# One PEER block kernel: thirty-two late tokens by gathered rows instead of sixteen, a 352-column score product, seven residual tiles on VectorE, and a new timetable of gathers

## The chip, the cores and the metric

The kernel is one program on one core of a Trainium2 chip. The metric is device time in microseconds (us), the median of three runs. TensorE's granted clock is 0.999 of full speed in the profiled execution.

## The reference

One trunk layer on 512 tokens of width 1024: a mixer (Mamba-2 and differential attention, not touched here), then PEER, then a gate. PEER is where the change lies, and it is the larger part of the time:

```python
q  = (xt @ wq).reshape(PEER_BLOCK, PEER_HEADS, 2, PEER_HALF)     # 8 heads, two halves
v1, i1 = top_k(q[:, :, 0] @ sub_k1.T, 16); v2, i2 = top_k(q[:, :, 1] @ sub_k2.T, 16)
top, pos = top_k(v1[..., None] + v2[..., None, :], 16)            # eidx = i1 * 128 + i2
g   = softmax(top)                                                # 128 experts for each token
act = gelu(einsum("td,thkd->thk", xt, expert_u[eidx]))
h  += einsum("thk,thkd->td", act * g, expert_v[eidx])
```

There are 16384 experts, a row of U and a row of V of 1024 floats each.

## The kernel before, in words

The 512 tokens are treated in three ways.

**384 tokens are "dense" for V**, in `DT = 384` columns. For 128 tiles of U (`n_steps`), each of 128 experts and 512 KB, TensorE computes the scores of those experts for the tokens (`score_products`): 24 matmuls per tile with `DS` columns, in three times eight. Eight use the high part of U and the high part of the tokens (L396), eight the high part of U and the low part of the tokens (L397), and, after a wait for `lo_ready`, eight use the low part of U (L402). The high part is a cast by ScalarE (`split`, L1769), the low part (the residual, raw minus high) a subtraction by GpSimd, called POOL below (`low_part`, L1606). ScalarE applies GELU (L1774), and SP stores 192 KB of activations per tile to DRAM. `raw`, `hi` and `lo` are rings of four tiles. ScalarE issues `split(n+2)` ahead of `gelu(n)`, so that the order on ScalarE is gelu(n), split(n+3), and the cast of tile n+3 starts as soon as TensorE is through with tile n.

**128 tokens** (the first block) are treated by gathered rows: for each of 128 pairs (head, rank) POOL issues an indirect DMA that fetches one row of U for each token (512 KB), into a ring of eight rows (`U_RING`), and VectorE multiplies it by the token's row in PSUM and adds up (`dot`, L1890).

**The last `XT` of the dense tokens** have their scores from gathered rows too ("late" pairs). The 128 pairs of 16 tokens are packed, 8 pairs at a time, into the 128 partitions, which makes `XK = 16` further gathers and dots; these dots have both operands in SBUF (`s_hn_x`). The dense score product then has only `DS = DT - XT = 368` columns. The results go through DRAM (`xa_dram`) and come back turned by strided DMAs (`take_back`), into the weights of the last steps.

The order of work is written out by hand. `due(n)` is the number of gathers that POOL has issued once it is through with tile n: after each `low_part(n)` it issues gathers up to `due(n)`. Before a gather it waits for the dot that read the same ring place eight gathers ago. VectorE takes its dots in places of their own: some between the pieces of the retrieval of blocks 1 to 3 (`DOTS_T`), then a free run up to `in_a`, then four and five around the softmax.

Tiles 2 to 71 have no other work on TensorE than the scores (and nine transposes after tile 69). At tiles 72 to 119 (the loop stage, 48 steps) VectorE makes one-hot matrices for 8 tokens per step (8 of L2017 and one of L2019) and one or two dots, and TensorE multiplies the one-hots (`spread_and_score`, L1690) ahead of each tile. Tiles 120 to 127 are scores alone again. In that tail SP issues, in this order, the stores of activations, the loads of the last U tiles, and the first loads of the gate weights (`load_weights`). Then comes the value stage: 32 groups of four V tiles, 72 matmuls of 512 columns each (L1706), with the row gathers of V beside it.

Of the kernel before, what the change touches and what calls it, by code (L numbers as in the profile page):

```python
# [10 lines left out]
F32 = mybir.dt.float32  # L11
# [4 lines left out]
ALU = mybir.AluOpType  # L16
# [17 lines left out]
PAIRS = PH * TOPK  # L34
# [31 lines left out]
UR = 4  # L66
WARM = 13
U_FIRST = 4
# [6 lines left out]
LOOP_A = 72  # L75
EXP_AT, TURN_AT = 64, 68
FIRST_GATHER = 10
KEPT = 2
DT = T - P
U_RING, U_AHEAD = 8, 4  # L80
DOTS_T, DOTS_M, DOTS_J = (0, 8, 10, 10), 12, 12
DOTS_FREE = 32
DOTS_EXP, DOTS_PRE = 4, 9
XT = 16
XG = P // XT
XK = PAIRS // XG
DS = DT - XT

# [1281 lines left out]
def experts_and_embedding(nc, new_sem, shared, io, act_dram, gate_dram, h_dram, e_dram, hx_dram, xi_dram, xa_dram, out):  # L1370
# [8 lines left out]
    n_steps = NK  # L1379
    turns = n_steps // UR  # L1380
    n_body = DT // (8 * STEP_TOK)
    LOOP_C = LOOP_A + 8 * n_body
    OUTS = 2 * (TB - 1)
    with ExitStack() as ctx:
# [30 lines left out]
        raw, hi, lo = (shared[k] for k in ("raw", "hi", "lo"))  # L1415
# [89 lines left out]
        v_rows = io["v_t"].rearrange("i p d -> (i p) d")  # L1505
        ident, iota = con[:, K_ID:K_ID + P], con[:, K_IOTA:K_IOTA + P]

        block = ctx.enter_context(nc.Block())

        @block.sync  # L1510
        def _(sp):
# [18 lines left out]
            def load_scores(it, s):  # L1530
                sp.wait_ge(lo_ready[s], it)
                sp.dma_start(raw[:, s, :], io["u_t"][it * UR + s]).then_inc(tile_loaded[s], 16)
                store_acts(it * UR + (s - UR), s, it)
# [9 lines left out]
                    load_scores(it, s)  # L1543
            load_scores(turns - 1, 0)
            load_scores(turns - 1, 1)
            for tile in range(2):
                sp.wait_ge(gates_stored[tile], 16 * (n_body - 1))
            for s in range(UR):
                sp.wait_ge(act_stored[s], 16)
            load_weights(0, 0, 0)  # L1550
            load_scores(turns - 1, 2)
            load_scores(turns - 1, 3)
            for s in range(UR):
                load_value(0, s)
                if s == 1:
# [42 lines left out]
        def _(pool):  # L1598
# [20 lines left out]
                                        bounds_check=NK * NK - 1).then_inc(row_loaded[s], 16)  # L1619
                pair_no += 1  # L1620

            def due(n):

                if n < EXP_AT:
                    return max(0, min(3 * (n - FIRST_GATHER + 1) // 2, in_a * (n - FIRST_GATHER + 1 + U_AHEAD) // (EXP_AT - FIRST_GATHER), in_a))
                if n < LOOP_A:
                    return in_a + 3 + 11 * (n - EXP_AT) // 8
                return min(PAIRS + XK, in_a + DOTS_PRE + 3 * (n - LOOP_A + 3) // 2)

            for n in range(n_steps):  # L1630
                if n >= U_FIRST:
                    low_part(n)
                while pair_no < due(n):
                    gather()
# [129 lines left out]
        def _(act):  # L1764
# [46 lines left out]
                        act.wait_ge(gates_copied[1], 8 * j + k + 1)  # L1811
                        act.dma_start(gate_dram[2 * j + tile], gtile[:, tile, :, :]).then_inc(gates_stored[tile], 16)

            steps(0)
            steps(1)
            for s in range(U_RING):
                act.wait_ge(dotted[s], x_till // U_RING + (s < x_till % U_RING))
            act.activation(x_dots[:, :], x_dots[:, :], ACT.Gelu).then_inc(x_gelu, 1)
            act.wait_ge(x_gelu, 1)
            act.dma_start(xa_dram, x_dots[:, :]).then_inc(xa_stored, 16)  # L1820
            steps(2)
            act.wait_ge(xa_stored, 16)

            def take_back(g):
                act.dma_start(x_acts[g * XK:(g + 1) * XK, :], xa_dram[g * XT:(g + 1) * XT, :].rearrange("t k -> k t"), allow_slow_non_contiguous=True).then_inc(xa_back, 16)

            steps(3, also=take_back)
            with act.Fori(4, n_body - 1) as j:
                steps(j)
            steps(n_body - 1, keep=True)  # L1830
            with act.Fori(LOOP_C // UR, turns - 1) as it:
                for s in range(UR):
# [53 lines left out]
        def _(dve):  # L1886
# [13 lines left out]
            def dot_of_pair(q):  # L1900
                late = x_from <= q < x_till
                if q == x_from:
                    dve.wait_ge(hx_loaded, 16 * XG)
                dot(q % U_RING, q // U_RING + 1, hn_x[:, :] if late else hn_dot, col(x_dots if late else dots, row_of(q)[1]))
# [73 lines left out]
            for t in range(1, TB):  # L1978
                retrieve(t, sum(DOTS_T[:t]), DOTS_T[t])
            dve.tensor_copy(x_ids[:, :], expert).then_inc(x_known, 1)  # L1980
            for q in range(sum(DOTS_T), in_a):
                dot_of_pair(q)
            done = TB * OPS

# [260 lines left out]
```

## Time and profile before

| What | us |
|---|---|
| median of 3 runs (lowest to highest) | 1562.83 (1560.61 to 1564.15) |
| the profiled execution's own time | 1560.82 |
| its span, first to last instruction | 1559.1 |
| TensorE busy | 1537.4 |
| VectorE busy | 1154.6 |
| POOL busy | 1068.5 |
| ScalarE busy | 628.1 |

TensorE's busy time is the union of modelled matmul spans, so the pace of a stage is read from where one group of matmuls starts after another, not from this total. The stages in the span: mixer and retrieval scores to 390; tiles 2 to 71 to 672.5; loop stage to 950.4; tail to 983; values to 1506; the gate to the end.

### The profile page before, as it was taken

The numbers are of one execution on the slowest core, as the hardware profiler recorded it, in microseconds if no ns is written. First come the engines' busy times: TensorE is split into PE (matmuls) and PEld (weight loads), VectorE is DVE, ScalarE is ACT, GpSimd is POOL, SyncE is SP. The second block draws the span as 40 slices with busy tenths as digits, with TensorE's granted clock in tenths as the row PEclk, the third lists the DMA queues.
The fourth block names the chain that finished last, engine by engine and source line by source line (L and its number), as shares of the span: only waits on it lengthen the run. The fifth ranks groups of instructions, "written<-read, shape, count | busy, mean of one in ns | idle before, by whom it ended". The sixth has DMA issues, their size and how long they took to land.

```text
span 1559.1 us, 24881 instructions
## 1 busy us (share of the span) xinstructions
PE 1537.4 (99%) x8622; PEld 1385.3 (89%) x8622; DVE 1154.6 (74%) x2386; ACT 628.1 (40%) x945; POOL 1068.5 (69%) x562
## 2 busy tenths in 40 slices
PE   9999999999999999999999999999999999999998
PEld 8976887788999999999999999888888888888887
DVE  7897573777999933399999992568677676776855
ACT  5335752202333333456555654433333333333331
POOL 6543315554598999888666665788878878788763
PEclk9999999999999999999999999999999999999999
DMA  7222103422599999899999997999999999999961
GB/s 285 106 74 102 69 28 125 143 89 96 176 360 339 317 335 332 300 312 362 360 345 351 360 328 227 338 349 366 356 370 358 358 357 346 351 342 349 344 228 54
DMA packets 169140, 420.46 MB, mean 270 GB/s; under 512 B 15968, under 2 KB 90208, under 8 KB 164336
## 3 DMA queue, kind: packets, MB, share of 16 engines
q1 hardware_dynamic: 125856, 256.02, 46.9%
q0 software_dynamic: 39168, 142.62, 25.6%
q10 hardware_dynamic: 4048, 21.01, 3.4%
q8 instruction: 31, 0.51, 0.1%
q14 instruction: 37, 0.30, 0.1%
HBM read 367.08 MB, written 52.51 MB: 269 GB/s over the span
## 4 chain that ended last, share of the span: by engine, by line
PE 66%; DVE 6%; issue 1%; POOL 1%; DMA 1%; ACT 0%; POOLq 0%
PE psum L1706 34%; PE psum L402 8%; PE psum L397 8%; PE psum L396 8%; PE psum L1690 5%; PE psum L257 1%; PE psum L248 1%; PE psum L258 1%; DVE psum L1961 1%; DVE s_gtile L1957 1%; DVE s_gtile L1959 1%; DMA s_late_rows<-in_u_rows,s_u_row 1%; DVE psum L1929 0%; POOL u_lo L1606 0%; DVE s_late_rows L1890 0%
## 5 line engine op out<-in xcount | busy, mean ns | idle before, releaser
L1606 POOL TENSOR_TENSOR u_lo<-u_raw,u_hi 128x1024 fp32r<-128x1024 f32 x220 | 551.7, 2508 | 175.0 <-ACT u_hi L1769 170.9
L1769 ACT CAST u_hi<-u_raw 128x1024 fp32r<-128x1024 f32 x252 | 263.7, 1048 | 291.0 <-PE psum L1706 256.4
L396 PE MATMUL psum<-hn_hi,u_hi 128*128 128x368 f32 x1024 | 340.6, 333 | 2.1 <-PEq L138 2.1
L397 PE MATMUL psum<-hn_lo,u_hi 128*128 128x368 f32 x1024 | 336.4, 329 | 0.0
L1706 PE MATMUL psum<-u_hi,s_whi 128*128 128x512 f32 x768 | 298.0, 389 | 0.9 <-ACT acts L1774 0.9
L1706 PE MATMUL psum<-u_lo,s_whi 128*128 128x512 f32 x768 | 298.0, 389 | 0.0
L1706 PE MATMUL psum<-u_hi,s_wlo 128*128 128x512 f32 x768 | 297.9, 389 | 0.0
L396 PEld LDWEIGHTS psum<-hn_hi,u_hi 128*128 128x128 f32 x1024 | 192.3, 188 | 2.4 <-issue 2.4
L402 PE MATMUL psum<-hn_hi,u_lo 128*128 128x368 f32 x1024 | 191.8, 329 | 0.7 <-POOL u_lo L1606 0.7
L397 PEld LDWEIGHTS psum<-hn_lo,u_hi 128*128 128x128 f32 x1024 | 192.2, 188 | 0.0
L1639 POOL DMA_INDIRECT s_vrows<-in_v_t,s_v_row x128 | 162.3, 1268 | 26.1 <-issue 24.5
L1774 ACT ACTIVATE acts<-psum 128x368 f32<-128x368 f32 x126 | 60.3, 478 | 292.3 <-PE psum L402 257.9
L2066 DVE SCALAR_TENSOR_TENSOR psum<-s_vrows,s_w,psum 128x1024 f32<-128x1024 f32 x127 | 162.7, 1281 | 19.3 <-DMA s_vrows<-in_v_t,s_v_row 10.2
L402 PEld LDWEIGHTS psum<-hn_hi,u_lo 128*128 128x128 f32 x1024 | 173.2, 188 | 1.2 <-POOL u_lo L1606 1.0
L229 POOL TENSOR_SCALAR m_w_hi<-m_w_raw 128x2048 fp32r<-128x2048 f32 (+1 forms) x23 | 44.0, 1912 | 186.6 <-PE psum L248 156.5
L1706 PEld LDWEIGHTS psum<-u_hi,s_whi 128*128 128x128 f32 x768 | 144.1, 188 | 31.0 <-issue 1.1
L1706 PEld LDWEIGHTS psum<-u_lo,s_whi 128*128 128x128 f32 x768 | 144.1, 188 | 30.1
L1706 PEld LDWEIGHTS psum<-u_hi,s_wlo 128*128 128x128 f32 x768 | 144.1, 188 | 29.9
L2035 DVE TENSOR_TENSOR scores<-scores,s_gtile 128x256 f32<-128x256 f32 x32 | 52.2, 1632 | 147.8 <-DMA scores<-gate_scratch 143.1
L2017 DVE TENSOR_SCALAR scores<-psum,scores 128x128 f32<-128x128 f32 x384 | 126.6, 401 | 7.7 <-PE psum L1690 7.7
L1890 DVE CUSTOM_DVE_ANT_0 s_late_rows<-s_late_rows,psum 128x1024 f32<-128x1024 f32 x64 | 76.9, 1216 | 49.9 <-DMA s_late_rows<-in_u_rows,s_u_row 49.9
L231 POOL TENSOR_TENSOR m_w_lo<-m_w_raw,m_w_hi 128x2048 fp32r<-128x2048 f32 (+1 forms) x23 | 106.3, 4623 | 1.9
(344 smaller groups left out, 2644.7 us busy)
## 6 DMA issues: line engine op xcount, KB each, us to landing
u_raw<-in_u_t SPq DMA_DIRECT2D x128, 512.0 KB
u_raw<-in_v_t SPq DMA_DIRECT2D x128, 512.0 KB
act_scratch<-acts SPq DMA_DIRECT2D x128, 192.0 KB
scores<-act_scratch SPq DMA_DIRECT2D x32, 768.0 KB
gate_scratch<-s_gtile ACTq DMA_DIRECT2D x10, 2048.0 KB
scores<-gate_scratch SPq DMA_DIRECT2D x32, 640.0 KB
m_w_raw<-in_w_in SPq DMA_DIRECT2D x9, 1024.0 KB, 4.8
m_w_raw<-in_w_q SPq DMA_DIRECT2D x8, 1024.0 KB, 4.8
```

Source lines behind the costliest of these rows:

```text
L231: pool.tensor_tensor(lo, raw, hi.bitcast(F32), ALU.subtract).then_inc(self.lo_ready[s], 1)
L396: pe.matmul(out, hi[:, d * P:(d + 1) * P], dense(hn_hi, d), start=(d == 0), stop=False)
L397: pe.matmul(out, hi[:, d * P:(d + 1) * P], dense(hn_lo, d), start=False, stop=False)
L402: last = pe.matmul(out, lo[:, d * P:(d + 1) * P], dense(hn_hi, d), start=False, stop=(d == DC - 1))
L1606: pool.tensor_tensor(lo[:, s, :], raw[:, s, :], hi[:, s, :].bitcast(F32), ALU.subtract).then_inc(lo_ready[s], 1)
L1639: pool.indirect_dma_start(vrows[:, k, :], None, v_rows, bass.IndirectOffsetOnAxis(ap=v_row[:, n:n + 1], axis=0), bounds_check=NK * NK - 1) ...
L1690: last = pe.matmul(psG[:, half, n, :], onehot[:, par, 0, 4 * half + n, :], onehot[:, par, 1, 4 * half + n, :], start=True, stop=True)
L1706: return pe.matmul(outs[o], ww[:, par, s, t * P:(t + 1) * P], vv[:, s, half * 512:(half + 1) * 512], start=start, stop=stop)
L1769: act.copy(hi[:, s, :], raw[:, s, :]).then_inc(hi_ready[s], 1)
L1890: dve.tensor_tensor_reduce(rows[s], rows[s], by, 1.0, 0.0, ALU.mult, ALU.add, into)\
L2017: dve.tensor_scalar(onehot[:, par, 0, n, :], iota_ps, col(pair[:, 0, :], t0 + n), col(pair[:, 1, :], t0 + n), ALU.is_equal, ALU.mult)
L2066: dve.scalar_tensor_tensor(hn_dot, vrows[:, k, :], w, hn_dot, ALU.mult, ALU.add).then_inc(vrow_added[k], 1)
```

## The change

- `XT` goes from 16 to 32. The dense product has 352 columns, there are 32 late gathers and dots instead of 16 (160 in all instead of 144), packed four pairs at a time; four `take_back` DMAs instead of eight, of twice the tokens each.
- `DOTS_FREE` goes from 32 to 38, so `in_a` goes from 60 to 66. The late dots take places 78 to 109 of the order of dots instead of 72 to 87, and ScalarE waits for them after the third round of `steps` instead of the second. The rest of those rounds is moved back by one.
- `due(n)` is new. Up to tile 41 it goes one gather per tile (two at tiles 11, 13, 24 and 41), from 42 to 63 it makes 30 gathers in 22 tiles, from 64 to 119 it has the cadence of before (12 in the eight tiles 64 to 71, then three per two tiles), and 10 gathers are left for tiles 120 to 125. Before, tiles 14 to 59 had about 1.11 per tile, 60 to 63 none and 120 to 127 none.
- The residuals of tiles 44, 47, 50, 53, 56, 59 and 62 (`DVE_LOW`) are made by VectorE. In its order they stand ahead of dot `due(n - 1)`, that is right behind the dot of the last gather that POOL issues at tile n-1.
- SP loads the last two U tiles ahead of its wait for the gates and of the first load of gate weights, and stores the activations in their places after it.

```diff
-DOTS_FREE = 32
+DOTS_FREE = 38
 DOTS_EXP, DOTS_PRE = 4, 9
-XT = 16
+FREE_AT = 41
+DVE_LOW = tuple(range(44, 64, 3))
+XT = 32
...
+        def due(n):
+
+            first = sum(DOTS_T) + U_RING
+            if n <= FREE_AT:
+                return max(0, min(3 * (n - FIRST_GATHER + 1) // 2, first * (n - FIRST_GATHER + 3) // (FREE_AT - FIRST_GATHER + 3)))
+            if n < EXP_AT:
+                return first + (in_a - first) * (n - FREE_AT) // (EXP_AT - 1 - FREE_AT)
+            if n < LOOP_A:
+                return in_a + 3 + 11 * (n - EXP_AT) // 8
+            if n < LOOP_C:
+                return in_a + DOTS_PRE + 3 * (n - LOOP_A + 3) // 2
+            return min(PAIRS + XK, in_a + DOTS_PRE + DOTS_J * n_body + 4 + 2 * (n - LOOP_C))
...
             load_scores(turns - 1, 1)
+            for s in range(2, UR):
+                sp.wait_ge(lo_ready[s], turns - 1)
+                sp.dma_start(raw[:, s, :], io["u_t"][n_steps - UR + s]).then_inc(tile_loaded[s], 16)
             for tile in range(2):
                 sp.wait_ge(gates_stored[tile], 16 * (n_body - 1))
             for s in range(UR):
                 sp.wait_ge(act_stored[s], 16)
             load_weights(0, 0, 0)
-            load_scores(turns - 1, 2)
-            load_scores(turns - 1, 3)
+            for s in range(2, UR):
+                store_acts(n_steps - 2 * UR + s, s, turns - 1)
...
             for n in range(n_steps):
-                if n >= U_FIRST:
+                if n >= U_FIRST and n not in DVE_LOW:
                     low_part(n)
...
-            steps(0)
-            steps(1)
+            for j in range(3):
+                steps(j)
...
-            steps(2)
+            steps(3)
             act.wait_ge(xa_stored, 16)
...
-            steps(3, also=take_back)
-            with act.Fori(4, n_body - 1) as j:
-                steps(j)
+            steps(4, also=take_back)
             steps(n_body - 1, keep=True)
...
+            def low_part(n):
+
+                s, it = n % UR, n // UR
+                dve.wait_ge(hi_ready[s], it + 1)
+                dve.wait_ge(tile_used[s], it)
+                dve.tensor_tensor(lo[:, s, :], raw[:, s, :], hi[:, s, :].bitcast(F32), ALU.subtract).then_inc(lo_ready[s], 1)
+
             for q in range(sum(DOTS_T), in_a):
+                for n in DVE_LOW:
+                    if q == due(n - 1):
+                        low_part(n)
                 dot_of_pair(q)
```

## Rows read from the trace of the kernel before

**Rows 1.** The chain that ended last, in order of time: start, us, what.

```profile
650.35 1.33 PE psum L402 x8
654.35 1.33 PE psum L402 x8
...
672.68 1.78 PE psum L1690 x16
677.13 1.33 PE psum L402 x8
...
682.92 1.33 PE psum L402 x8
...
983.31 522.52 PE psum L1706 x2304
```

**Rows 2.** Busy time by window: its us, PE, PEld, DVE, ACT, POOL, clock, DMA, GB/s.

```profile
464.00:472.00 8.00, 8.00 (x50) 7.92 (x49) 7.97 (x59) 3.46 (x5) 7.62 (x5) 1.00 1.00 386
...
550.00:664.00 114.00, 114.00 (x688) 113.97 (x687) 41.61 (x65) 43.49 (x60) 101.90 (x60) 1.00 0.92 323
672.00:820.00 148.00, 148.00 (x1028) 148.00 (x1027) 147.31 (x316) 89.33 (x105) 111.52 (x66) 1.00 0.94 344
...
946.00:983.00 37.00, 36.44 (x220) 36.13 (x219) 7.01 (x10) 15.40 (x22) 21.62 (x9) 1.00 0.76 253
983.00:1506.00 523.00, 522.69 (x2308) 432.82 (x2309) 372.54 (x264) 179.85 (x162) 420.66 (x226) 1.00 0.98 347
```

**Rows 3.** Timeline of POOL, tiles 14 and 32 to 33.

```profile
436.77 2.40 POOL L1606 TENSOR_TENSOR u_lo<-u_raw,u_hi 128x1024 fp32r<-128x1024 f32 x1
...
510.65 2.42 POOL L1606 TENSOR_TENSOR u_lo<-u_raw,u_hi 128x1024 fp32r<-128x1024 f32 x1
513.23 1.04 POOL L1618 DMA_INDIRECT s_late_rows<-in_u_rows,s_u_row  x1 [0.16 <-issue]
514.58 1.01 POOL L1618 DMA_INDIRECT s_late_rows<-in_u_rows,s_u_row  x1 [0.30 <-issue]
515.61 2.42 POOL L1606 TENSOR_TENSOR u_lo<-u_raw,u_hi 128x1024 fp32r<-128x1024 f32 x1
519.25 2.42 POOL L1606 TENSOR_TENSOR u_lo<-u_raw,u_hi 128x1024 fp32r<-128x1024 f32 x1
```

**Rows 4.** Timeline of TensorE: residual products of tiles 2, 33 and 64.

```profile
393.07 0.33 PE L402 MATMUL psum<-hn_hi,u_lo 128*128 128x368 f32 x1
```
```profile
518.08 0.43 PE L402 MATMUL psum<-hn_hi,u_lo 128*128 128x368 f32 x1 [0.68 <-POOL u_lo L1606]
```
```profile
642.19 0.49 PE L402 MATMUL psum<-hn_hi,u_lo 128*128 128x368 f32 x2
```

**Rows 5.** Timeline of POOL, tile 64: its residual and three gathers.

```profile
633.21 2.40 POOL L1606 TENSOR_TENSOR u_lo<-u_raw,u_hi 128x1024 fp32r<-128x1024 f32 x1 [1.60 <-ACT u_hi L1769]
635.76 1.04 POOL L1618 DMA_INDIRECT s_late_rows<-in_u_rows,s_u_row  x1 [0.15 <-issue]
...
638.42 1.01 POOL L1618 DMA_INDIRECT s_late_rows<-in_u_rows,s_u_row  x1 [0.30 <-issue]
```

**Rows 6.** Timeline of VectorE: dots of the first and third of those gathers.

```profile
642.49 1.22 DVE L1890 CUSTOM_DVE_ANT_0 s_late_rows<-s_late_rows,psum 128x1024 f32<-128x1024 f32 x1 [16.64 <-DMA s_late_rows<-in_u_rows,s_u_row]
...
646.33 1.22 DVE L1890 CUSTOM_DVE_ANT_0 s_late_rows<-s_late_rows,psum 128x1024 f32<-128x1024 f32 x1 [0.58 <-DMA s_late_rows<-in_u_rows,s_u_row]
```

**Rows 7.** The value stage's residuals on VectorE: ns min/median/max, first and last start.

```profile
L2072 DVE TENSOR_TENSOR u_lo<-u_raw,u_hi x32: 1208/1213/2495, 985.2 to 1490.7; 128x1024 fp32r<-128x1024 f32 x32
```

**Rows 8.** Timeline of POOL, tile 69's gather, and VectorE after it.

```profile
657.91 1.31 POOL L1618 DMA_INDIRECT s_late_rows<-in_u_rows,s_u_row  x1 [0.16 <-issue]
```
```profile
664.81 1.22 DVE L1890 CUSTOM_DVE_ANT_0 s_late_rows<-s_late_rows,psum 128x1024 f32<-128x1024 f32 x1 [1.93 <-DMA s_late_rows<-in_u_rows,s_u_row]
```

**Rows 9.** Timeline of VectorE in the loop stage, late dots.

```profile
727.81 1.98 DVE L1890 CUSTOM_DVE_ANT_0 s_late_rows<-s_late_rows,s_hn_x 128x1024 f32<-128x1024 f32 x1
...
734.54 2.59 DVE L1890 CUSTOM_DVE_ANT_0 s_late_rows<-s_late_rows,s_hn_x 128x1024 f32<-128x1024 f32 x1
737.07 0.08 DVE L1890 DVE_READ_ACCUMULATOR2_ANT s_x_dots<- 128x1 f32 x1
737.07 2.63 DVE L2017 TENSOR_SCALAR scores<-psum,scores 128x128 f32<-128x128 f32 x8
739.63 1.20 DVE L2019 TENSOR_TENSOR scores<-con,psum 128x1024 f32<-128x1024 f32 x1
740.76 1.21 DVE L1890 CUSTOM_DVE_ANT_0 s_late_rows<-s_late_rows,s_hn_x 128x1024 f32<-128x1024 f32 x1
```

**Rows 10.** Timeline of POOL in the loop stage, same stretch.

```profile
733.65 2.41 POOL L1606 TENSOR_TENSOR u_lo<-u_raw,u_hi 128x1024 fp32r<-128x1024 f32 x1 [1.64 <-ACT u_hi L1769]
```

**Rows 11.** The tail: SP's first weights load, VectorE's use of it.

```profile
960.01 0.57 SPq L1528 DMA_DIRECT2D scores<-gate_scratch  x1
```
```profile
966.95 0.43 DVE L2035 TENSOR_TENSOR scores<-scores,s_gtile 128x256 f32<-128x256 f32 x1 [26.89 <-DMA scores<-gate_scratch]
```

More of the change, by code:

```diff
@@ L1620, in gather @@
                 pair_no += 1
[L1622 to L1628, printed above, removed]
             for n in range(n_steps):
-                if n >= U_FIRST:
+                if n >= U_FIRST and n not in DVE_LOW:
                     low_part(n)
@@ L1820, in _ @@
             act.dma_start(xa_dram, x_dots[:, :]).then_inc(xa_stored, 16)
-            steps(2)
+            steps(3)
             act.wait_ge(xa_stored, 16)
             def take_back(g):
+                if g >= XG:
+                    return
                 act.dma_start(x_acts[g * XK:(g + 1) * XK, :], xa_dram[g * XT:(g + 1) * XT, :].rearrange("t k -> k t"), allow_slow_non_contiguous=True).then_inc(xa_back, 16)
-            steps(3, also=take_back)
-            with act.Fori(4, n_body - 1) as j:
-                steps(j)
+            steps(4, also=take_back)
             steps(n_body - 1, keep=True)
```

## The prediction

> **What bounds the kernel now.** I first read the chain of work that ended last. From tile 2 to the value stage it is TensorE alone, at a constant pace: a score tile every 4.00 us outside the loop stage, a step every 5.79 us in it, and the 2304 matmuls of the value stage in 522.52 us [rows 1]. The windows by stage say the same: TensorE is busy all the time from 550 to 820 [rows 2]. They also show who is near behind. Up to tile 71 POOL is busy 101.90 of 114 us, in the first half of the loop stage VectorE is busy 147.31 of 148 us, and the 16 DMA engines show a share of 0.92 to 0.98 in every stage but the tail [rows 2]. So a cheaper score tile gives time directly, until POOL, VectorE or the DMA engines take over. Then I read the timelines of POOL and TensorE side by side, to see how far ahead each residual is of the matmul that needs it.
>
> **The gain on TensorE.** A matmul's pitch is 4.00 us / 24 = 166.7 ns at 368 columns and 522.52 / 2304 = 226.8 ns at 512 columns [rows 1]: 0.418 ns per column, so 16 columns less are 6.7 ns less, 160.0 ns, and a tile takes 3.84 us, 0.16 less. Is there a floor? The 16 matmuls of 128 columns take 1.78 us, 111 ns each [rows 1]. A line from there to 368 columns has only 0.23 ns per column, which would give 0.09 us per tile. I take 0.16, because 352 lies next to the 368 and in line with the 512, and keep 0.09 as the low end. Tiles 2 to 127 are 126: 126 x 0.16 = 20.2 us (low end 11.3). The value stage keeps its 512 columns and its number of matmuls, and gains nothing.
>
> **POOL up to tile 43.** POOL takes 519.25 - 515.61 = 3.64 us for a residual and one gather, and 515.61 - 510.65 = 4.96 us with two: 1.3 us for the second [rows 3]. Before, tile 33's residual was ready at 518.03 and TensorE waited 0.68 us for it; its product came 0.9 us late against the 4.00 us grid (393.07 + 31 x 4.00 = 517.07) [rows 3, 4]. The new timetable has four gathers fewer by tile 33, so this 0.9 us goes. At the new pace, tile 14 is the tight one: its residual is ready at 436.77 + 2.40 = 439.17 [rows 3], its product is wanted at 393.07 - 0.1 + 12 x 3.84 = 439.0. That is 0.1 us of wait. From there on POOL gains 3.84 - 3.65 = 0.19 us per tile and loses 1.3 at each of the two doubles (24 and 41), so at tile 43 it is 29 x 0.19 - 2.6 = 2.9 us ahead. VectorE's ten dots per retrieved block find their rows in time either way, since their gathers are 10 us or more ahead of them.
>
> **Seven residuals on VectorE.** Here a new wait arises. VectorE makes residual n behind the dot of the last gather of tile n-1. Count from the end e of POOL's residual n-1. The gather starts at e + 0.16. Its row comes 6.7 us later when it is the first of a burst (635.76 to 642.49), and the dot of the third began 7.9 us after its issue (638.42 to 646.33) [rows 5, 6]. Bursts of three it will be, as POOL, relieved of residual n, goes straight on to the gathers of tile n. Then 1.15 us for the dot and 1.21 us for the residual [rows 6, 7]: e + 9.2 after a single gather (n = 44, 47, 50), and e + 0.16 + 1.34 + 7.3 + 2.4 = e + 11.2 after a double (53, 56, 59, 62). When is it wanted? With POOL in full lead the residual n-1 is ready 6.2 us ahead of its product. (Tile 64 shows 642.19 - 635.61 = 6.6 [rows 4, 5]; over two tiles the new pace takes 0.3 of it.) One tile of 3.84 us on top makes e + 10.0. So the singles just pass, the doubles miss by 1.2 us. Tile 44 is worse, as POOL's lead there is only 2.9: wanted at e + 6.7, ready at e + 9.2, a miss of 2.5. A miss also gives the next of the seven, three tiles on, that much more room, since the cast it hangs on is tied to an earlier tile. So I count 2.5 at 44, 1.2 at 53, 1.2 at 59. To this comes the port. A late dot in the loop stage, with both operands in SBUF, that begins while POOL makes a residual ends one dot's length after that residual: 734.54 took 2.59 us, ending at 737.13, where POOL's residual ended at 736.06 [rows 9, 10]. VectorE's residuals in the value stage go up to 2.50 us beside their median of 1.21 for the same reason [rows 7]. I add 0.6 on three of them, some 2 us. Sum: 7 us. Bounds: if rows come in 5 us, about 0.5 (tile 44 alone); if in 8 and the port is always taken, 12.
> The Trainium skill, in SBUF — State Buffer, section Who interferes with whom, says that a VectorE instruction with two SBUF inputs and a GpSimd instruction that reads SBUF exclude each other for the whole instruction. The rows on the late dots agree. By the rule alone each of the seven would wait up to a whole residual of POOL.
>
> **Gathers and DMA, tiles 42 to 71.** Between two of the seven POOL makes two residuals and four or five gathers, some 10.5 us of its 11.5, and stays in lead. From 64 to 71 it is over its pace by 12 gathers: 8 x 3.65 + 4 x 1.3 = 34.4 us against 31.7 with the transposes. It has the lead for that. A tile moves 524 KB of U, 197 KB of activations and 1.36 x 524 KB of rows, 1.44 MB: 374 GB/s at 3.84 us. The most that eight microseconds show is 386 GB/s at a share of 1.00, and the mean of long stretches is 323 to 347 [rows 2]. The stalls above stretch the mean tile to some 4.07 us and the demand down to 353 GB/s. So I cost the DMA engines at nothing beyond the 7 us, and keep them as a rival.
>
> **The start of the loop stage.** VectorE's first one-hot waits for dot 74, whose row is gathered at tile 69. Before, that gather went out at 657.91 and the dot began at 664.81 [rows 8], after which copies and a one-hot set (3.7 us) ended 1.7 us ahead of TensorE's need at 672.7 [rows 1]. Before, POOL was 4.4 us ahead at tile 69. Now the two gathers of tile 63 and the twelve after it leave 2.0, so all this comes 2.4 us later against TensorE, and TensorE's own need comes 0.4 earlier. I count 1.2 us (0 to 3).
>
> **The late dots in the loop stage.** Without contention VectorE needs per step 740.76 - 737.07 = 3.69 us for the one-hots and 1.5 dots of 1.15: 5.42 us [rows 9]. The new step is 5.79 - 0.16 = 5.63. The stretch by POOL's residuals is some 0.46 per step on average (over the eleven steps with late dots), which makes 5.88, more than TensorE's step. There are now 21 such steps instead of 11. I expect this to hold itself in check. As VectorE falls back, its first dot slides behind the end of POOL's residual, as at 740.76, which took 1.21 [rows 9], and the stretch is gone. I count 1 us; nothing (0) and 21 x 0.25 = 5 us are its ends.
>
> **The tail.** Ten gathers fall on tiles 121 to 125. POOL loses 1.1 us per tile of a lead of 6.2: hidden. They add 5.2 MB to a stage that runs at a share of 0.76 [rows 2]; the first weights, issued at 960.01 and used at 966.95 [rows 11], are wanted only by ScalarE's cast around 979.8, so some 10 us cover the later load, as they do for the two U tiles that are put ahead. The last dots end some 1 us ahead of the cast. 0.5 us (0 to 3). Nothing is gained here by the order of SP's loads, since TensorE's pitch was 4.00 us before. The 4-byte `take_back` packets double to 4096; they ride beside the gathers and I cost them at nothing, as the loop stage has DMA share to spare (0.94) [rows 2].
>
> **Sum.** -20.2 - 0.9 + 0.1 + 7 + 1.2 + 1 + 0.5 = -11.3 us. Against the profiled execution's 1560.82 that is 1549.5. The median of the runs is 2.0 higher, so the median should be 1551.5.
>
> **The rivals.**
> - Nothing new waits: the rows come in 5 us, and VectorE's slack is enough. Then -20.2 - 0.9 + 1, 1542.7 on the scale of the median. For it: TensorE never waits today. Against: tile 44's margin. 0.15.
> - The DMA engines bound tiles 42 to 71. If they give no more than 350 GB/s, these tiles need 22 x 1.44 + 8 x 1.51 = 43.7 MB, 125 us, where TensorE needs 116: 9 us. The loop stage moves 2.03 MB per step (a quarter of a 2.1 MB gate store besides), 5.79 us at 350 GB/s: nothing gained there at the worst. With 9 us and half of the loop stage's 7.9 lost, besides the 2.7 of the last three terms, the gain is some 5 us: 1558. For it: shares near 1. Against: 386 GB/s in eight microseconds [rows 2]. 0.2. The Trainium skill (DMA: Bandwidth & Descriptors, section Bandwidth) puts the HBM limit of a core at about 358 GB/s; by that figure the case would be an estimated 2 us better. The row with 386 exceeds it.
> - Slower: VectorE becomes the bound of the loop stage. If each late first dot meets a whole residual, as the one that took 2.59 did, it is stretched by 1.38: a step takes 6.80, 1.17 over TensorE's, 25 us over 21 steps, which ends at 1565 with the rest at its small end. It decides from about 1.0 per step. Against: it happened once in eleven. 0.06.
> - My forecast: 0.5. The rest, 0.09, goes to a mix near no change (residuals missing by 3 us each).
>
> The range 1543 to 1560 leaves out part of the first, of the worst DMA case and the slow side. Measurements can tell about 0.2% (3.1 us) here. Faster by more: 0.83; within: 0.1; slower: 0.07.
>
> **What would show it.** Matmuls of L402 with 352 columns in groups 3.84 us apart, 5.63 in the loop stage. TensorE waiting for VectorE's residual at tile 44 by 2 us or more, and at some of the others. VectorE's residuals longer than 1.3 us where POOL is in one. TensorE waiting for VectorE's one-hot at step 0. If TensorE has no waits, or if ScalarE's casts wait for U tiles by many microseconds (the DMA case), or if TensorE waits for one-hots all through tiles 74 to 95, I am wrong in that step.

## The result: slower by 0.3%, and where the time of the profiled execution went

| | before | after |
|---|---|---|
| median of 22 runs each (lowest to highest), us | 1561.77 (1560.49 to 1567.72) | 1567.33 (1561.90 to 1569.49) |
| ratio, 95% interval | | 1.0027 [1.002, 1.0034] |
| profiled execution, own time and span, us | 1560.82, 1559.1 | 1568.41, 1566.6 |

The forecast was 1551.5, the range 1543 to 1560. It was wrong, with its sign. I go by the profile: what TensorE waits for, where on its time line that lies, and what the engine waited for was doing.

First TensorE's waits in the kernel after (engine, line, tile, what it waited for: us in total, times, longest). Before, none of these four waits was above 0.9 us in sum.

```profile
PE psum L404 <- DVE u_lo L1996: 11.9, 4, 6.6
PE psum L1716 <- ACT acts L1784: 4.3, 1, 4.3
PE psum L404 <- POOL u_lo L1624: 2.8, 3, 1.4
PE psum L1700 <- DVE scores L2039: 2.8, 1, 2.8
```

L404 is the residual product (L402 before), L1996 VectorE's new residual, L1700 the product with the one-hots (L1690 before), L1716 the value stage (L1706 before).

The chain that ended last, near the end of the tail (start, us, what). It answers to [rows 1].

```profile
941.73 1.28 PE psum L404 x8
...
947.36 1.28 PE psum L404 x8
...
960.67 1.28 PE psum L404 x8
964.51 1.29 PE psum L404 x8
966.31 4.01 SPq L1529
970.36 6.81 SPq L1529
978.22 7.94 DMA u_raw<-in_v_t
989.32 524.08 PE psum L1716 x2304
```

The pace is as forecast: 964.51 - 960.67 = 3.84 us per tile, and in the loop stage 947.36 - 941.73 = 5.63. But the chain leaves TensorE for two stores on SP's queue and the transfer of a V tile. The value stage begins at 989.32 instead of 983.31, and its 2304 matmuls take 524.08 us instead of 522.52 [rows 1].

The windows of the kernel after, which answer to [rows 2] (its us, PE, PEld, DVE, ACT, POOL, granted clock, DMA share, GB/s):

```profile
550.00:664.00 114.00, 102.06 (x608) 100.91 (x609) 63.27 (x89) 37.63 (x53) 86.65 (x56) 0.96 0.91 323
560.00:570.00 10.00, 5.61 (x21) 5.61 (x22) 7.84 (x10) 1.40 (x2) 7.08 (x5) 0.66 0.79 282
672.00:820.00 148.00, 145.19 (x1026) 144.49 (x1025) 144.16 (x313) 86.11 (x102) 123.84 (x70) 1.00 0.95 351
946.00:983.00 37.00, 37.00 (x238) 37.00 (x237) 12.84 (x22) 13.11 (x18) 28.06 (x18) 1.00 0.93 333
988.00:992.00 4.00, 2.68 (x6) 2.15 (x7) 3.36 (x2) 1.16 (x3) 2.18 (x1) 0.65 1.06 388
```

From 550 to 664 TensorE is busy 102.06 of 114 us, and its mean clock is 0.96: some of the waits are followed by a stretch at the lower level of 1.2 GHz. Followed tile by tile (start of one residual product after the other, against 3.84 and 5.63), the span divides so:

| Term | forecast, us | profiled executions, us |
|---|---|---|
| narrower products, tiles 2 to 127 | -20.2 | -20.0 |
| the wait at tile 33 | -0.9 | -0.9 |
| tiles 11 to 41 | +0.1 | +3.0 |
| tiles 42 to 71, with the seven residuals | +7 | +18.5 |
| start of the loop stage | +1.2 | +3.0 |
| late dots in the loop stage | +1 | +0.4 |
| tail and start of the value stage | +0.5 | +5.0 |
| tile 2 starts earlier (391.75 for 393.07) | 0 | -1.3 |
| sum | -11.3 | +7.7 (the spans differ by 7.5) |

**Tile 44**, the largest piece, in the kernel after. First POOL (start, us, what, the idle time before it and what ended it):

```profile
542.48 1.04 POOL L1636 DMA_INDIRECT h<-in_u_rows,s_u_row  x1 [0.16 <-issue]
546.39 1.01 POOL L1636 DMA_INDIRECT s_more_row<-in_u_rows,s_u_row  x1 [2.87 <-DVE s_dots L1900]
...
551.03 2.43 POOL L1624 TENSOR_TENSOR u_lo<-u_raw,u_hi 128x1024 fp32r<-128x1024 f32 x1
553.62 1.04 POOL L1636 DMA_INDIRECT s_late_rows<-in_u_rows,s_u_row  x1 [0.16 <-issue]
```

Then VectorE, and TensorE's residual products of tiles 43 and 44:

```profile
546.75 0.29 DVE L1990 CAST s_x_ids<-psum 128x128 uint32<-128x128 int32 x1
...
560.20 1.22 DVE L1900 CUSTOM_DVE_ANT_0 s_late_rows<-s_late_rows,psum 128x1024 f32<-128x1024 f32 x1 [2.22 <-DMA s_late_rows<-in_u_rows,s_u_row]
561.35 0.08 DVE L1900 DVE_READ_ACCUMULATOR2_ANT s_dots<- 128x1 f32 x1
561.35 2.99 DVE L1996 TENSOR_TENSOR u_lo<-u_raw,u_hi 128x1024 fp32r<-128x1024 f32 x1
```
```profile
553.80 1.44 PE L404 MATMUL psum<-hn_hi,u_lo 128*128 128x352 f32 x8
564.39 2.72 PE L404 MATMUL psum<-hn_hi,u_lo 128*128 128x352 f32 x8 [6.59 <-DVE u_lo L1996]
```

Read from the bottom. The product of tile 44 was wanted at 553.80 + 3.84 = 557.6 and waited until 564.39. The residual ended at 561.35 + 2.99 = 564.34. With e, the end of POOL's residual 43, at 551.03 + 2.43 = 553.46, it was ready at e + 10.9, where I had e + 9.2: the row came after 560.20 - 553.62 = 6.6 us as expected, but the residual took 2.99 us instead of 1.21. It was wanted at e + 4.2, where I had e + 6.7: POOL's lead of 2.9 us had gone at tile 42, where its gather stood 2.87 us for a place in the ring, that is for a dot of VectorE. And VectorE was late because the last instruction of its retrieval (L1990, L1980 before) began at 546.75, not at 536.44 as before. I call that start the end of the retrieval below.

Why that? The small subtraction in the retrieval (two operands in SBUF), four times, in the kernel before (L1950) and after (L1960); ns min/median/max, first and last start:

```profile
L1950 DVE TENSOR_TENSOR s_found<-s_gtile x4: 284/346/1144, 403.9 to 513.6; 128x128 f32<-128x128 f32 x4
```
```profile
L1960 DVE TENSOR_TENSOR s_found<-s_gtile x4: 1527/2772/3299, 402.7 to 520.9; 128x128 f32<-128x128 f32 x4
```

An instruction of 0.28 us takes up to 3.30. The second of the four, beside POOL:

```profile
440.43 3.28 DVE L1960 TENSOR_TENSOR s_found<-s_gtile 128x128 f32<-128x128 f32 x1
```
```profile
440.06 1.04 POOL L1636 DMA_INDIRECT s_late_rows<-in_u_rows,s_u_row  x1 [0.16 <-issue]
441.12 2.42 POOL L1624 TENSOR_TENSOR u_lo<-u_raw,u_hi 128x1024 fp32r<-128x1024 f32 x1
```

Each of the four ended 0.1 to 0.2 us after the end of a residual of POOL. Two of them (2.27 and 1.53 us) began inside that residual. The two longest (3.28 and 3.30 us) began 0.7 us ahead of it, while POOL was in a gather; why they didn't get through in that time stays open, since one in the kernel before took 0.29 us beside a gather. In sum the four took 10.4 us instead of 2.1, and all dots of a late block behind them are late as well.

**The tail** of the kernel after: SP's issues, and ScalarE behind them.

```profile
962.85 1.18 SPq L1563 DMA_DIRECT2D u_raw<-in_u_t  x2
964.28 0.39 SPq L1542 DMA_DIRECT2D scores<-act_scratch  x1
964.72 0.79 SPq L1543 DMA_DIRECT2D scores<-gate_scratch  x1
966.31 10.86 SPq L1529 DMA_DIRECT2D act_scratch<-acts  x2
977.22 0.46 SPq L1533 DMA_DIRECT2D u_raw<-in_v_t  x1
```
```profile
984.38 1.05 ACT L1779 CAST u_hi<-u_raw 128x1024 fp32r<-128x1024 f32 x1 [6.57 <-DMA u_raw<-in_v_t]
985.33 0.46 ACT L1784 ACTIVATE acts<-psum 128x352 f32<-128x352 f32 x1
```

SP stands 10.86 us in the issue of two stores (a single one took 0.34 to 0.36 at the same place before). V tile 0 goes out at 977.22 (before: 967.37), its cast waits 6.57 us, and the activations of tile 126 and all else the value stage needs stand behind that cast in ScalarE's order.

### The profile page after: what moved, and what is told of

Read it like the earlier page. It is cut to its first block, busy times and chain, and to the rows that moved or that the text cites. A ratio compares the mean times of both kernels' runs of the same rounds, so it can differ in the third digit from the quotient of the medians.

```text
span 1566.6 us, 24934 instructions
## 1 busy us (share of the span) xinstructions
PE 1525.1 (97%) x8622; PEld 1370.3 (87%) x8622; DVE 1195.9 (76%) x2425; ACT 627.3 (40%) x945; POOL 1079.2 (69%) x571
## 4 chain that ended last, share of the span: by engine, by line
PE 56%; DVE 10%; issue 3%; DMA 3%; POOL 2%; SPq 1%; ACT 0%; POOLq 0%
PE psum L1716 33%; PE psum L1700 6%; PE psum L404 5%; PE psum L399 5%; PE psum L398 5%; DVE s_gtile L1967 1%; DVE psum L1971 1%; DVE s_gtile L1969 1%; DVE s_late_rows L1900 1%; DMA h<-in_u_rows,s_u_row 1%; PE psum L259 1%; PE psum L250 1%; PE psum L260 1%; DMA s_late_rows<-in_u_rows,s_u_row 1%; DVE h L1900 1%
## 5 line engine op out<-in xcount | busy, mean ns | idle before, releaser
L1624 POOL TENSOR_TENSOR u_lo<-u_raw,u_hi 128x1024 fp32r<-128x1024 f32 x213 | 529.7, 2487 | 162.9 <-ACT u_hi L1779 159.3
L398 PE MATMUL psum<-hn_hi,u_hi 128*128 128x352 f32 x1024 | 333.7, 328 | 2.1 <-PEq L140 2.1
L399 PE MATMUL psum<-hn_lo,u_hi 128*128 128x352 f32 x1024 | 329.6, 324 | 0.0
L1716 PE MATMUL psum<-u_hi,s_whi 128*128 128x512 f32 x768 | 299.3, 391 | 4.3 <-ACT acts L1784 4.3
L1716 PE MATMUL psum<-u_lo,s_whi 128*128 128x512 f32 x768 | 298.3, 389 | 0.0
L1716 PE MATMUL psum<-u_hi,s_wlo 128*128 128x512 f32 x768 | 298.0, 389 | 0.0
L404 PE MATMUL psum<-hn_hi,u_lo 128*128 128x352 f32 x1024 | 188.1, 326 | 14.7 <-DVE u_lo L1996 11.9
L1649 POOL DMA_INDIRECT s_vrows<-in_v_t,s_v_row x128 | 167.3, 1307 | 27.7 <-issue 24.2
L404 PEld LDWEIGHTS psum<-hn_hi,u_lo 128*128 128x128 f32 x1024 | 169.0, 190 | 17.0 <-DVE u_lo L1996 13.1
L1716 PEld LDWEIGHTS psum<-u_hi,s_whi 128*128 128x128 f32 x768 | 144.8, 189 | 34.7 <-issue 4.6
L1716 PEld LDWEIGHTS psum<-u_lo,s_whi 128*128 128x128 f32 x768 | 144.5, 188 | 30.0
L1716 PEld LDWEIGHTS psum<-u_hi,s_wlo 128*128 128x128 f32 x768 | 144.1, 188 | 30.1
L1784 ACT ACTIVATE acts<-psum 128x352 f32<-128x352 f32 x126 | 58.5, 464 | 277.3 <-PE psum L404 277.3
L2055 DVE TENSOR_TENSOR scores<-scores,s_gtile 128x256 f32<-128x256 f32 x32 | 46.2, 1443 | 131.7 <-DMA scores<-gate_scratch 131.7
L1816 ACT COPY s_gtile<-psum 128x512 f32<-128x512 f32 x96 | 100.2, 1156 | 2.5 <-PE psum L1700 2.5
```

Source lines behind the costliest of these rows:

```text
L398: pe.matmul(out, hi[:, d * P:(d + 1) * P], dense(hn_hi, d), start=(d == 0), stop=False)
L399: pe.matmul(out, hi[:, d * P:(d + 1) * P], dense(hn_lo, d), start=False, stop=False)
L404: last = pe.matmul(out, lo[:, d * P:(d + 1) * P], dense(hn_hi, d), start=False, stop=(d == DC - 1))
L1624: pool.tensor_tensor(lo[:, s, :], raw[:, s, :], hi[:, s, :].bitcast(F32), ALU.subtract).then_inc(lo_ready[s], 1)
L1649: pool.indirect_dma_start(vrows[:, k, :], None, v_rows, bass.IndirectOffsetOnAxis(ap=v_row[:, n:n + 1], axis=0), bounds_check=NK * NK - 1) ...
L1716: return pe.matmul(outs[o], ww[:, par, s, t * P:(t + 1) * P], vv[:, s, half * 512:(half + 1) * 512], start=start, stop=stop)
```

## The experiments

Each is timed beside the kernel before on the same chip; ratios are to that, with their 95% interval. The times of one kernel spread more than before's do, so that one profile is not its median; where I speak of an effect's size, it comes from the ratios.

**One part alone: 352 columns.** The kernel before with

```diff
+DM = 352
...
-    dense = lambda t, d: t[:, d, P:P + DS]
+    dense = lambda t, d: t[:, d, P:P + DM]
```

and the same width in PSUM and in the activations.

> The kernel before with 352 instead of 368 columns in the score product and its GELU, and nothing else of the change. It leaves out the scores of 16 tokens, whose activations are set to one. If the pitch of the matmuls follows the columns, score tiles come every 3.84 us and the ceiling of the gain is 20 us; POOL's timetable of before is too dense for that pace up to tile 20, so I expect TensorE to wait some 3 us there and the run to be 14 to 17 us faster than before. If instead the DMA engines are the next bound (rival), the tiles from 14 to 71 keep a pace near 3.95 to 4.0 us and the run is less than 8 us faster.

Measured: 1549.51 us (1547.67 to 1552.95), 0.9919 [0.9902, 0.9937]. The pitch is 3.84. From tile 2 to 127 it is 11.1 us shorter than before, not 20: the timetable of before, at the new pace, makes TensorE wait for POOL in seven of the tiles 12 to 33 (4.8 us, and some 2.6 us more beside these waits). So a new timetable was needed, but the columns alone, with the old one, were worth 12.7 us, less than the 14 to 17 expected and more than the rival's 8. The rest of the change, with the sixteen late gathers that this run leaves out, takes more than that back.

**Who makes the residuals.** The kernel after with POOL making all of them:

```diff
-DVE_LOW = tuple(range(44, 64, 3))
+DVE_LOW = ()
```

> The changed kernel with all residuals on POOL and the same timetable of gathers. POOL needs 22 x 3.65 + 8 x 1.3 = 91 us for tiles 42 to 63 and has 84 plus its lead. If VectorE's lateness (theory: its retrieval ends 10 us later, and its residuals stand behind the dots) costs 16 us in tiles 44 to 60, this run waits instead some 3 to 8 us for POOL and is 8 to 12 us faster than the changed kernel, so 4 to 8 us faster than before. If the late rows and full DMA queues are the cause whoever makes the residuals (rival), ScalarE's casts wait for U tiles and the time stays within 3 us of the changed kernel.

Measured: 1560.34 us (1555.37 to 1567.52), 0.9988 [0.9971, 1.0005]. TensorE waits 5.7 us for POOL, in eight tiles. So giving seven residuals to VectorE, in the places they have, made the kernel some 6 us slower than leaving them with POOL (8 to 12 were expected).

**Where they stand in VectorE's order.** The kernel after with each residual behind the dot of the last gather of tile n-2:

```diff
-                    if q == due(n - 1):
+                    if q == due(n - 2):
```

> The changed kernel with VectorE's residual n in front of dot due(n-2) instead of due(n-1), so one tile's gathers less stand before it. Theory (the place in VectorE's order costs the time): the waits at tiles 50, 53 and 59 go (6 us and the 1.7 us of lower clock after 59), the one at 44 shrinks from 6.6 us by one or two dots to about 4 to 5, and the run is 6 to 9 us faster than the changed kernel. Rival (the port is what holds VectorE's residuals): nearly the same waits, within 2 us of it.

Measured: 1554.77 us (1551.55 to 1560.40), 0.9958 [0.9945, 0.9971]: 0.69% below the ratio of after, 10.8 us. TensorE's waits in this kernel:

```profile
PE psum L1716 <- ACT acts L1784: 4.7, 1, 4.7
PE psum L1700 <- DVE scores L2039: 3.1, 1, 3.1
...
PE psum L404 <- POOL u_lo L1624: 1.4, 2, 0.8
```

No wait for a residual of VectorE is left among them (0.3 us are lost at tile 44). It wasn't VectorE's load that cost the time, but the place: behind a row that was asked for only 4 us before the residual was wanted (553.62 for 557.6 at tile 44). This run also shows how much the DMA engines give in these tiles:

```profile
550.00:664.00 114.00, 113.05 (x704) 112.44 (x702) 73.75 (x96) 45.93 (x62) 99.70 (x63) 1.00 1.00 373
```

TensorE keeps its pace with 373 GB/s at a share of 1.00. What is left stands at the start of the loop stage and of the value stage. At the first one the tile took 6.1 us too long with a wait of 3.1: in the windows behind it the granted clock is 0.53 for 5 us, then 0.79.

```profile
665.00:670.00 5.00, 3.71 (x17) 3.71 (x18) 5.00 (x12) 1.70 (x2) 4.50 (x4) 0.53 0.89 316
670.00:675.00 5.00, 5.00 (x28) 5.00 (x27) 5.00 (x12) 1.14 (x2) 3.50 (x3) 0.79 0.70 219
```

**The order of loads in the tail.** The kernel after with the last two U tiles loaded in their old places:

```diff
-            for s in range(2, UR):
-                sp.wait_ge(lo_ready[s], turns - 1)
-                sp.dma_start(raw[:, s, :], io["u_t"][n_steps - UR + s]).then_inc(tile_loaded[s], 16)
...
-            for s in range(2, UR):
-                store_acts(n_steps - 2 * UR + s, s, turns - 1)
+            load_scores(turns - 1, 2)
+            load_scores(turns - 1, 3)
```

> The changed kernel with SP's order of before in the tail: the last two U tiles behind the first weights. Theory: it is the ten gathers in the tail that fill the queues, and the order matters little: SP still stands at a store, the value stage starts within 1 us of the changed kernel's. Rival: the two U tiles ahead of the weights block SP's queue; without them the value stage starts some 3 us earlier, and the run is 3 to 5 us faster than the changed kernel.

Measured: 1572.74 us (1562.09 to 1576.63), 1.007 [1.005, 1.0089], 0.43% or 6.7 us slower than after; both theories had it equal or faster. Its profiled execution was the shortest of six and shows how: the load stands 6.95 us in SP's issue, ScalarE's cast of tile 126 waits, and behind it TensorE waits 4.1 us in the tail.

```profile
972.08 1.04 ACT L1776 CAST u_hi<-u_raw 128x1024 fp32r<-128x1024 f32 x1 [9.69 <-DMA u_raw<-in_u_t]
```

So this part of the change is worth something, in a kernel that has gathers in the tail.

**The port.** The kernel after with the small subtraction's first operand copied to PSUM ahead of it:

```diff
-                did(dve.tensor_tensor(found[:, t, 2, :].rearrange("p (h k) -> p h k", h=PH), top[:, :, :],
+                did(dve.tensor_copy(leftf[:, :, :], top[:, :, :]))
+                me.settle()
+                did(dve.tensor_tensor(found[:, t, 2, :].rearrange("p (h k) -> p h k", h=PH), leftf[:, :, :],
...
```

> The changed kernel, with the small subtraction of the retrieval (128 x 128, both inputs in SBUF, 10.4 us for four of them in the changed kernel's profile, 2.1 before) fed by a copy in PSUM instead, so that it has one input in SBUF. Theory (a port shared with POOL makes these four wait, and the 10 us of delay of the retrieval are what makes TensorE wait 6.6 us at tile 44): each of the four takes under 0.4 us, the retrieval ends by 540, the wait at tile 44 is under 2 us, and the run is 6 to 9 us faster than the changed kernel. Rival (the retrieval is late because its rows come late): the subtractions are short, the dots wait for DMA instead, and tile 44 waits as before.

Measured: 1565.44 us (1560.05 to 1568.29), 1.002 [1.0009, 1.0032]. The four subtractions took 0.29 us each, and the retrieval ended at 538.96. TensorE's wait at tile 44 fell from 6.59 to 3.8, but not away:

```profile
PE psum L404 <- DVE u_lo L1998: 8.8, 3, 3.8
```

The mechanism is shown, its weight is small: the ratio is 0.0007 (about 1 us) below that of after, inside the intervals, where 6 to 9 us were expected. The profiles suggest why: the stretch comes and goes. In this stretch of the time line the work is the same in after and in seven of the experiments. The retrieval ended at 546.75 in after and at 547.46 in one of them (activations first), at 543.37 with POOL making all residuals, and between 536.15 and 538.23 in the other five. The four subtractions took up to 3.29 us in the second, and none took more than 2.35 in the other six. So the profile of after shows one of the bad cases, and the copy can only give what the mean of them costs.

**The tail's gathers.** The kernel after without the last eight (head, rank) pairs of the first 128 tokens.

```diff
-            return min(PAIRS + XK, in_a + DOTS_PRE + DOTS_J * n_body + 4 + 2 * (n - LOOP_C))
+            return min(PAIRS + XK - 8, in_a + DOTS_PRE + DOTS_J * n_body + 4 + 2 * (n - LOOP_C))
...
```

> The changed kernel without the last eight of its gathers and dots, which leaves 2 of 10 gathers for tiles 120 to 125. It leaves out eight of the 128 pairs of the first 128 tokens. Theory (these gathers fill the DMA queues, SP stands 11 us in an issue, and the first V tile comes late): the value stage starts 1 us after the last score instead of 4.3, without the lower clock, and the run is 4 to 6 us faster than the changed kernel. Rival (the two U tiles ahead of the weights do it): the wait stays above 3 us.

Measured: 1562.42 us (1555.80 to 1568.07), 1.0004 [0.9987, 1.0021]: 0.23% or 3.6 us below after, with intervals that just touch. SP's issue of the two stores shrinks from 10.86 to 4.20, V tile 0 goes out at 966.95, and the wait at L1716 falls to 0.9, the value of before. From 960 to 980 the DMA share is 0.98 with 320 GB/s, where after has 1.05 and 390 from 966 to 983.

```profile
962.71 4.20 SPq L1529 DMA_DIRECT2D act_scratch<-acts  x2
966.95 0.43 SPq L1533 DMA_DIRECT2D u_raw<-in_v_t  x1
```

**The start of the loop stage.** Residuals two tiles earlier as above, and the last two dots ahead of the loop stage put behind the first one-hot set:

```diff
-            for q in range(in_a + DOTS_EXP, in_a + DOTS_PRE):
+            for q in range(in_a + DOTS_EXP, in_a + DOTS_PRE - 2):
...
+                if step_no == 0:
+                    for q in range(c0 - 2, c0):
+                        dot_of_pair(q)
```

> The kernel of the run two tiles earlier, with the last two dots ahead of the loop stage put behind its first set of one-hots. There TensorE waited 3.1 us for VectorE at step 0 and ran at half clock for 4 us after it, 6.1 us in all. Theory (the one-hots stand behind a dot whose row comes late): this goes to 0 to 1 us, and the run is 4 to 6 us faster than that one, near 1549. Rival (VectorE is simply full there): the wait comes back at step 1 to 3, less than 2 us are gained.

Measured: 1551.67 us (1547.92 to 1554.72), 0.9935 [0.9921, 0.995], 3.6 us below the kernel with the earlier residuals alone, with intervals that just touch. The wait went from step 0 (3.1 us) to step 3 (2.5 us), with 2 us less lost in all. So a different order moves the wait more than it removes it; that VectorE simply has too much to do in the first steps fits that, but wasn't tried by itself. Another cause that fits stands in the kernel after, just ahead of this place:

```profile
676.00:680.00 4.00, 4.00 (x27) 4.00 (x26) 2.72 (x7) 1.52 (x2) 3.81 (x3) 1.00 1.04 411
```
```profile
677.24 1.22 DVE L1900 CUSTOM_DVE_ANT_0 h<-h,psum 128x1024 f32<-128x1024 f32 x1 [1.48 <-DMA h<-in_u_rows,s_u_row]
```

The DMA engines are at a share of 1.04 with 411 GB/s, and the row of the last dot ahead of the one-hots, gathered at 669.68, was there 7.6 us later, where the forecast had 6.9. No run takes this load away. With the copy to PSUM as well:

> The one before, with the subtraction fed from PSUM as well. Theory: where the retrieval happened to run free of POOL, this adds nothing in the profile, but it takes out the chance of it, so that the times of all runs lie closer together and their median is 0 to 4 us lower. Rival (the port has no part in the spread): spread and median as without it.

Measured: 1552.27 us (1548.54 to 1554.27), 0.9941 [0.9928, 0.9954]. Not told apart from the one before.

**Why V tile 0 is late.** On that basis, once with the load of V tile 0 ahead of the two stores on SP, and once with ScalarE's activations of tile 126 ahead of the cast of V tile 0:

```diff
+            load_value(0, 0)
             for s in range(2, UR):
                 store_acts(n_steps - 2 * UR + s, s, turns - 1)
...
```
```diff
             for s in range(UR):
+                if s == 2:
+                    gelu(turns - 1, s)
                 split(turns - 1 + (s + 2) // UR, (s + 2) % UR)
...
```

> The kernel of the run before (residuals two tiles earlier, first one-hot set ahead of two dots; ratio 0.9935, profiled span 1549.5 us), and besides SP issues the load of V tile 0 ahead of the last two stores of activations instead of behind them. Theory A (the wait at the start of the value stage is V tile 0 that lands late, because its issue stands on SP behind stores that the ten tail gathers hold up): V tile 0 is issued at about 951 instead of 960.3 us, ScalarE's cast of it starts as soon as its buffer is free, and the wait of 3.2 us with about 1 us of lower clock behind it goes: 3 to 4 us less, ratio 0.9910 to 0.9915. Theory B (the DMA engines themselves are full there, the order on SP does not matter): the load is issued earlier and lands at 966 or later all the same, no change, ratio 0.9935.

> The same kernel as the basis (ratio 0.9935), and besides ScalarE makes the activations of tile 126 ahead of the cast of V tile 0 instead of behind it. Theory A (V tile 0 is late, and all of ScalarE's work behind it: two casts of V, one of weights, the activations of tile 127): only one activation of 0.46 us leaves the row behind the late cast, so the wait goes from 3.2 to some 2.7 us, ratio 0.993 to 0.9935. Theory C (the wait is made by ScalarE's order, the activations of tile 126 behind a cast that waits for its tile): the wait goes almost whole, 3 us less, ratio 0.9915.

Measured: 1552.95 us, 0.9945 [0.9929, 0.996], and 1553.24 us, 0.9940 [0.9922, 0.9958]. Neither helps. In the first, SP's issue and ScalarE's cast were:

```profile
950.96 0.34 SPq L1533 DMA_DIRECT2D u_raw<-in_v_t  x1
951.35 7.29 SPq L1529 DMA_DIRECT2D act_scratch<-acts  x3
```
```profile
965.03 1.05 ACT L1781 CAST u_hi<-u_raw 128x1024 fp32r<-128x1024 f32 x1 [4.25 <-DMA u_raw<-in_v_t]
```

The load goes out 9.3 us earlier than in its basis (960.29) and is there 2.4 us earlier (965.03 for 967.45), 14 us after its issue; 1.2 of the 2.4 is only that all of this execution lies that much ahead. So it isn't SP's order. The windows of the tail point to what it is: the 20 us up to the last residual product in this kernel (966.56) and in the one before the change (980.94).

```profile
946.00:966.00 20.00, 20.00 (x126) 20.00 (x125) 7.12 (x11) 5.89 (x10) 14.74 (x9) 1.00 1.04 388
```
```profile
960.00:980.00 20.00, 20.00 (x122) 20.00 (x121) 5.31 (x9) 7.30 (x11) 12.01 (x6) 1.00 0.93 311
```

A share of 1.04 with 388 GB/s for 20 us, where the kernel before had 0.93 with 311: the DMA engines are full. That what is issued there waits for them is a reading; the run with eight gathers less, in which the wait went, bears it out. In the second, ScalarE's activations of tile 126 waited 4.00 us for the store of tile 122's, which lay in the same jam.

**All four together** (earlier residuals, one-hots first, copy to PSUM, both orders of the tail):

> Residuals two tiles earlier, first one-hot set ahead of two dots, the retrieval's subtraction fed by a copy in PSUM, V tile 0 loaded ahead of the stores, activations of tile 126 ahead of the cast of V tile 0. If the four causes add up as the single runs show them, only the wait for one-hots at tile 75 (2.3 us) and the start waits are left: span about 1543, time about 1546, ratio 0.990. If something else takes over at the start of the value stage (the weights, or V tiles 2 and 3 behind the stores), 1549 or more.

Measured: 1550.33 us (1546.48 to 1552.41), 0.9922 [0.9906, 0.9937], the lowest of the kernels that compute the whole result, though its interval overlaps those of the four before it. The four edits do not add up to the 0.990 expected; TensorE's two large waits stay:

```profile
PE psum L1718 <- ACT acts L1786: 3.8, 1, 3.8
PE psum L1702 <- DVE scores L2046: 2.1, 1, 2.1
```

That is 1.05% faster than the changed kernel and 0.78% faster than before, as much as the narrower columns alone gave (0.9919, with the scores of 16 tokens left out).

## Why the prediction was wrong, step by step

- **The gain on TensorE**: right. The pitch is 160 ns at 352 columns, no floor, 20 us.
- **POOL up to tile 43**: the step that failed first. The wait at tile 33 went, as said. But "VectorE's ten dots per retrieved block find their rows in time either way" looked at rows only, not at when VectorE gets to its dots. A dot that comes late holds a place of the ring, and through it POOL. The lead of 2.9 us was 0.3 when tile 44 came (553.80 - 553.46). Tiles 11 to 15 cost 2.3 us instead of 0.1, with waits for POOL of 0.78 and 0.62; with the small subtraction fed from PSUM they cost 0.4 and, with all four edits, 0.6, so they too seem to come from the port.
- **Seven residuals on VectorE**: the mechanism was right (residual behind a row of the tile before, port on top), and the size was off, 18.5 for 7 us in the profile. At tile 44, 6.75 for 2.5: 2.5 of it from the lead, 1.7 from the port. At 53 and 59, 2.6 for 1.2 each. Tile 42, where the lead went, took 1.6 too long, and tile 50 0.6. 4.0 us is what no term of mine had: the lower clock behind the waits at 44 and 59. The port itself made the seven residuals 7.4 us longer in sum than seven times 1.21, where I had added 2. With the retrieval on time (the run with the copy) the wait at 44 was still 3.8. By the ratios the place alone is worth 10.8 us, and VectorE's part in the residuals, as placed, costs 6 us more than it saves. This is the term that was mis-sized most.
- **The start of the loop stage**: 3.0 for 1.2, at the upper end of its bounds. The first one-hot set began at 679.64. The gathers ahead of it are as many as I counted; the last of their rows took 7.6 us for 6.9, and by the experiment, order gives back only a part.
- **Late dots in the loop stage**: right. 0.4 us for 1; the pace of 5.63 held, and VectorE stayed busy 144.16 of 148 us. The slower rival, which needed a stretch of each step, did not occur: the kernel is slower, for which I had 0.07, but not on the way that I had named for it.
- **The tail**: failed. I spread 5.2 MB over a stage at a mean share of 0.76, but its second half had been at 0.91 before already (966 to 983). After, the gathers go out from 947 to 973, and their end meets the weights, two U tiles and V tile 0: the share from 966 to 983 is 1.05, with 390 GB/s. The stores and V tile 0 stood in that jam, and with eight of the ten gathers left out the wait fell from 4.3 to 0.9 us. "Some 10 us cover the later load" named the cover for the weights, not for V tile 0, which had none. 3.4 us until the value stage starts, and 1.6 of lower clock in it. "Nothing is gained here by the order" failed too: the old order costs 6.7 us more.
- **The DMA rival** did not occur in tiles 42 to 71 as I had put it: ScalarE's casts waited 1.3 us in all for U tiles from 550 to 664, and with the residuals two tiles earlier these tiles kept the pace with 373 GB/s, above the 350 of the rival. The loop stage kept its pace with 351 GB/s at a share of 0.95. Full engines showed in the tail (390 GB/s at 1.05) and for some microseconds ahead of the loop stage (411 at 1.04). The 2 us that I gave in this rival for the second, higher rate was low: 43.7 MB take 2.8 us less by it.

Two things stay open. The difference was to be -11.3 us. The medians differ by +5.6, and the ratio 1.0027 makes it +4.2; I go by the ratio, as for the experiments, so 15.5 us are to be explained. The place of the residuals (10.8), the one-hots (3.6) and the tail's gathers (3.6) make 18.0 us where I had 7, 1.2 and 0.5: 9.3 of the 15.5. The copy to PSUM gives about 1 more. Some 5 us are not placed by any run. Each of these terms has an interval of a few microseconds, so part of the 5 may be spread. And no run tried fewer bytes in the tail with the whole result computed.

## What to carry to other kernels

When work is given to an engine that has slack, ask where in its order it stands, and what the instruction ahead of it waits for: here the place was worth more than the work. A ring ties its two users together in both directions, so a consumer that is late by some microseconds takes the lead of the producer. And the mean DMA share of a stage says nothing of its last 20 us; count what must land there, and what goes out ahead of it.

## What the runs showed of the hardware

- TensorE's granted clock fell to the lower level after some waits: after 6.59 us at tile 44 it was 0.50 from 564 to 568, after 4.3 us 0.65 from 988 to 992. After the wait of 2.46 us at tile 59 it was 0.72 from 632 to 636, after one of the same 2.46 us at tile 53 it stayed, and so it did after 2.76 us at the start of the loop stage (1.00 from 684 to 694). So the length of a wait alone does not tell. Each fall cost 1.6 to 3 us. The wait of 3.1 us in the kernel with earlier residuals cost 6.1 in all.
- A VectorE subtraction of 128x128 with both operands in SBUF takes 0.28 us alone and up to 3.30 where it ends with a residual of POOL (2.42 us), and one operand in PSUM takes this away (0.29, four times of four). The Trainium skill, SBUF — State Buffer, section Who interferes with whom, states this lock for the whole instruction; the trace agrees, but for the 0.7 us by which the two longest began ahead of the residual.
- SP can stand 10.86 us in issuing two stores while the DMA engines show a share of 1.05; with the load ahead of the stores, V tile 0 was there 14 us after its issue.
